# State-space coefficients made earlier, around the last heads of the recurrence, and the first query product in the common form

## The reference, cut to what matters

```python
# first layer: the modulated input times w_in, whose first columns are the queries
widths = (A_WIDTH, A_KV_WIDTH, A_KV_WIDTH, A_WIDTH, B_WIDTH, B_WIDTH, B_WIDTH, B_WIDTH)
q, k, v, g_a, xb, b_g, c_g, g_b = split_cols(modulate(x, shift, scale) @ w_in, widths)
# second layer: the recurrence's readout, head by head, then the output product
on = o * lax.rsqrt(jnp.mean(o * o, axis=-1, keepdims=True) + RMS_EPS) * g_norm
return (on.transpose(0, 2, 1, 3).reshape(B, L, H * dv) * jax.nn.silu(g)) @ w_out
# third layer: coefficients of the state-space mixer, from parameters alone
A = lax.complex(a_re, a_im)
dt = jnp.exp(log_dt)[:, None]
a_bar = jnp.exp(A * dt)
b_bar = ((a_bar - 1.0) / A)[..., None] * lax.complex(b_re, b_im)
bu = jnp.einsum('gpc,bsgc->bsgp', b_bar, u)
```

## Time and profile before

| | |
|---|---|
| median of 3 runs | 2365.18 us (2356.86 to 2365.84) |
| the profiled execution | 2361.89 us |
| its span, first to last instruction | 2360.1 us |
| mean granted TensorE clock | 0.974 |
| PE busy | 2196.2 us (93%) |
| DVE / ACT / POOL busy | 1076.5 / 668.6 / 801.4 us |

### The profile page before, as it was taken

How to read it: one execution, slowest core, us unless ns; L and a number is a source line. 1 busy time by engine, 2 the same in 40 slices (tenths; PEclk the granted TensorE clock), 3 DMA queues, 4 the chain that set the end, 5 groups by cost and what they waited for, 6 DMA issues and landing times. The chain is left out here.

```text
span 2360.1 us, 28075 instructions
## 1 busy us (share of the span) xinstructions
PE 2196.2 (93%) x11735; PEld 1766.8 (75%) x11735; DVE 1076.5 (46%) x1653; ACT 668.6 (28%) x1031; POOL 801.4 (34%) x382
## 2 busy tenths in 40 slices
PE   5999898989999999998978899999998999999997
PEld 3887777866676868886845678888887578888886
DVE  2114664653666565667896543111126664111114
ACT  3223223324545454642102432000013443010101
POOL 1422013401323322335400015544544255554453
PEclk7999999999999999998999999999999999999999
DMA  9332114422111111113111112323222222232322
GB/s 305 74 108 72 55 54 113 121 90 89 36 37 36 36 36 36 37 54 99 41 36 54 54 54 80 99 90 107 90 89 90 90 88 73 89 107 90 98 90 81
DMA packets 174797, 187.47 MB, mean 79 GB/s; under 512 B 25600, under 2 KB 153936, under 8 KB 174544
## 3 DMA queue, kind: packets, MB, share of 16 engines
q1 hardware_dynamic: 164720, 175.42, 23.8%
q10 hardware_dynamic: 9376, 8.16, 1.3%
q0 software_dynamic: 576, 2.10, 0.2%
HBM read 183.56 MB, written 2.10 MB: 79 GB/s over the span
## 5 line engine op out<-in xcount | busy, mean ns | idle before, releaser
L3022 POOL TENSOR_TENSOR weights_lo<-weights_raw,weights_hi 128x2048 fp32r<-128x2048 f32 (+1 forms) x102 | 462.5, 4534 | 851.1 <-ACT weights_hi L1443 654.9
L700 PE MATMUL ring<-input_hi,weights_hi 128*128 128x512 f32 x784 | 305.6, 390 | 3.3 <-POOL weights_lo L3022 3.0
L701 PE MATMUL ring<-input_lo,weights_hi 128*128 128x512 f32 x784 | 305.3, 389 | 0.0
L702 PE MATMUL ring<-input_hi,weights_lo 128*128 128x512 f32 x784 | 305.3, 389 | 0.0
L2864 DVE CAST weights_hi<-weights_raw 128x2048 fp32r<-128x2048 f32 (+1 forms) x72 | 87.7, 1218 | 366.1 <-PE ring L702 173.9
L3010 POOL TENSOR_TENSOR h_w<-h_p 128x512 f32<-128x512 f32 x56 | 72.6, 1297 | 413.9 <-PE ring L1031 307.8
L1004 PE MATMUL obank<-acts,weights_raw 128*128 128x512 f32 x384 | 176.6, 614 | 0.8 <-issue 0.8
L700 PEld LDWEIGHTS ring<-input_hi,weights_hi 128*128 128x128 f32 x784 | 147.2, 188 | 35.0 <-issue 4.6
L702 PEld LDWEIGHTS ring<-input_hi,weights_lo 128*128 128x128 f32 x784 | 147.2, 188 | 30.6
L701 PEld LDWEIGHTS ring<-input_lo,weights_hi 128*128 128x128 f32 x784 | 147.2, 188 | 30.2
L1013 PE MATMUL obank<-weights_raw,acts 128*128 128x256 f32 x640 | 143.2, 381 | 0.0
(11 more groups left out here) (474 smaller groups left out, 4409.8 us busy)
## 6 DMA issues: line engine op xcount, KB each, us to landing
weights_raw<-in_w_ada SPq DMA_DIRECT2D x24, 1024.0 KB, 5.3
weights_raw<-in_ffn_w_gate SPq DMA_DIRECT2D x22, 1024.0 KB, 5.2
weights_raw<-in_ffn_w_up SPq DMA_DIRECT2D x22, 1024.0 KB, 5.1
weights_raw<-in_w_in_c SPq DMA_DIRECT2D x20, 1024.0 KB, 5.2
weights_raw<-in_ffn_w_down SPq DMA_DIRECT2D x16, 1024.0 KB, 5.0
weights_raw<-in_w_in_ab SPq DMA_DIRECT2D x9, 1024.0 KB, 7.1
weights_raw<-in_ev_w_in SPq DMA_DIRECT2D x8, 1024.0 KB, 5.4
weights_raw<-in_od_w_in SPq DMA_DIRECT2D x8, 1024.0 KB, 5.6
```

Of the source, the lines that this page charges most:

```text
L700: pe.matmul(o, hi[:, k, ms], xh[:, k, t0:t0 + n], start=k == 0, stop=False)
L701: pe.matmul(o, hi[:, k, ms], xl[:, k, t0:t0 + n], start=False, stop=False)
L702: last = pe.matmul(o, lo[:, k, ms], xh[:, k, t0:t0 + n], start=False, stop=k == KD - 1)
L3022: pool.tensor_tensor(W_LO[slot][:, 0:kt, :], WR[:, slot, 0:kt, :], w_hi[:, 0:kt, :], ALU.subtract).then_inc(sem("w_lo"), 1)
```

## The change

It does two separate things. The first undoes the product of its own for `q0`: `q0` and `q1` both go through `split_f`, which waits for hi and lo weights first and then does the three matmuls k by k, each k of the first column tile behind its `h_lo`.

The second reorders DVE, ACT and POOL at the end of the recurrence. `s5_angles` loses its first part, which becomes `s5_columns`. The pieces of the diff are, in order: PE's list, ACT's list (between the root and `hi_upto("y11.0")` stand, as before, four loads of B and C and two of norm rows, which ACT issues), DVE's list, and POOL's.

```diff
-            hi, lo = split_chunk("q0", head_columns(0, 0), wait_lo=False)
...
-            split_f("q1", head_columns(0, 1), "a", True, H_HI, H_LO)
+            for c in range(2):
+                split_f(f"q{c}", head_columns(0, c),
+                        "a", True, H_HI, H_LO, "a", None if c else sem("h_lo"))
...
             heads_hi(0)
+            act.wait_ge(*read_of("s5rows"))
+            act.activation(pr(2), pr(2), ACT.Exp).then_inc(sem("s5_dt"), 1)
             heads_hi(1)
             heads_hi(2)
             hi_upto("y10.1")
+            act.wait_ge(sem("s5_ang"), 1)
+            act.activation(pr(5), pr(3), ACT.Exp)
+            act.activation(pr(2), pr(3), ACT.Exp, scale=float(CH))
+            act.activation(pr(6), pr(6), ACT.Sin)
+            act.activation(pr(7), pr(7), ACT.Sin).then_inc(sem("s5_sc"), 1)
             root(range(3, 4), 2)
...
+            hi_upto("y11.0")
             heads_hi(3)
-            pr = lambda k: SPR[:, k, :]
-            act.wait_ge(*read_of("s5rows"))
-            act.activation(pr(2), pr(2), ACT.Exp).then_inc(sem("s5_dt"), 1)
-            hi_upto("y11.0")
-            act.wait_ge(sem("s5_ang"), 1)
...
             hi_upto("y11.1")
...
                     heads_lo(1)
                     heads_lo(2)
-            inside(HEADS // HH - 1)
-            normed_heads(3)
-            heads_lo(3)
+            s5_angles()
+            inside(HEADS // HH - 1)
+            normed_heads(3)
+            s5_weights()
+            heads_lo(3)
+            s5_columns()
+            s5_inputs()
...
             tile_norms(y1_norm, 1, C_DIAG, HT, V_NPRE)
-            s5_weights()
-            s5_inputs()
...
+                lo_upto("y11.0")
+                s5_powers()
                 lo_upto("y11.1")
-                s5_powers()
                 s5_tables()
```

More of the change, by code:

```diff
@@ L587, in gemm_f, with split_chunk @@
                 used_with_unit()
-            def split_chunk(name, pieces, kt=KD, by="a", wait_lo=True):
+            def split_chunk(name, pieces, kt=KD, by="a"):
                 chunk(pieces, kt)
@@ L601, in split_chunk @@
                 pe.wait_ge(hi_done, len(hi_list))
-                if not wait_lo:
-                    return w_hi, w_lo
                 by_v = sum(x in split_no for x in LO_BY_V)
@@ L1776, in _ @@
             act.wait_ge(*fill_of(f"oi{LAST}"))
+            pr = lambda k: SPR[:, k, :]
             hi_upto("y10.0")
@@ L2510, in s5_angles, with s5_columns @@
             def s5_angles():
+                dve.wait_ge(sem("s5_dt"), 1)
+                mul(pr(3), pr(0), pr(2))
+                mul(pr(4), pr(1), pr(2))
+                sine_args(pr(4), pr(6), pr(7), pr(8), "s5_ang")
+                dve.wait_ge(sem("s5_ang"), 1)
+            def s5_columns():
                 dve.wait_ge(sem("s5_c_in"), 32)
@@ L2517, in s5_angles @@
                 ins.then_inc(sem("s5_cexp"), 1)
[L2518 to L2522, removed]
             def s5_weights():
```

## The result

The changed kernel takes 2371.19 us (median, 2367.03 to 2375.86), the kernel before in the same comparison 2364.52 us (2356.86 to 2365.84). The ratio is 1.0035 with a 95% interval from 1.0021 to 1.0049: about 8 us slower (5 to 12); the two medians alone differ by 6.7. The profiled execution took 2370.28 us, its span is 2368.5 us, against 2361.89 and 2360.1 before.

What follows compares the result with a forecast made beforehand. PE, busy 93% of the span, was taken as the bound, so only its waits could move the end. The terms 2.6 + 6.0 + 1.7 - 1.5 = +8.8 us, from 2365.2, gave 2374.0 us, range 2362 to 2381.

Steps and rivals of the forecast that it cites:

- Part 1: First query product: `q1` starts later, first column tile going k by k behind `h_lo`; +1.6 to +3.9 us, taken as +2.6.
- The clock cost that I added: First query product: second column tile may start at low clock, up to 1.7 us, plus 0.6 for the last three matmuls.
- Part 2: Output product, third tile: PE waits for L2389, delayed by angle operations that POOL stops; +6.0 us, bounds +1.4 and +6.0.
- the row that I had taken for the case: DVE's operation at 1078.81 in the earlier trace, taken as the same code beside the same POOL instruction: 4.57 us for 0.18.
- The clock behind it: Output product, behind the stall: PE's matmuls run at a low clock; +1.7 us, bounds 0 and 3.3.
- Rival C: Low clock lasts two stretches behind the output product's stall, and `q0`'s second column tile starts low; +11.7 us, chance 0.17.
- The rest of part 2: Last heads, joins, lo part of `y11.1`: reordered work hidden by PE's shift; cost 0, at worst +1 us at joins.
- 2.3 us to spare: POOL's lo part of `y11.1`, behind the powers, done at 1100.2; PE needs it at 1102.5, so cost 0.
- at worst 1 us: Second half's first joins: `s5_columns` and `s5_inputs` standing ahead of them cost 0, at worst +1 us.
- 3.7 us of cover: Last heads, without the stall: normed at about 1069.5, ahead of PE's turn at 1073.16, so 3.7 us of cover.
- Part 3: Behind the norm: PE's 1.53 us wait for DVE's powers vanishes; -1.5 us.
- Rivals A and B: Output product's third tile: A, small stall, +2.5 us, chance 0.18; B, no ring wait, faster, -1.4 us, chance 0.10.

Runs made afterwards that it cites:

- q_alone: Kernel before with only the first query product changed (both chunks through `split_f`); 2367.4 us, ratio to before 1.0003.
- pool_away: Changed kernel with ACT's hi part of `y10.1` behind the wait for the sine arguments, so POOL's lo part comes later; 2368.67 us, ratio to before 1.0010.
- reader_first: Changed kernel with DVE's `inside(3)`, the reader of `oo3`, ahead of `s5_angles`; ratio to before 1.0013.
- coef_alone: Changed kernel with the old `q0` product, so only the coefficients are moved; 2371.18 us, ratio to before 1.0023.
- pool_order: Changed kernel with POOL's old order: lo part of `y11.1`, then powers, then tables; ratio to before 1.0021.
- final: Changed kernel with old `q0`, `inside(3)` ahead of `s5_angles`, ACT's root and last heads earlier, readout directly behind DVE's powers; 2356.97 us, ratio to before 0.9970.
- final_old: `final` with POOL's old order (both lo parts, then powers, then tables); 2356.35 us, ratio to before 0.9964.
- mended: Changed kernel with the edits of `reader_first` and `pool_order` and the old `q0`; 2364.34 us, ratio to before 1.0009.
- readout_early: `mended` with `s5_readout` moved from behind the first scan step to directly behind DVE's `s5_powers`; 2355.06 us, ratio to before 0.9958.

## Why the prediction came out, point by point

The forecast was +8.8 us, 2374.0; measured were 2371.19 us and +8 (5 to 12) by the ratio. The stall, its place and what ends it came as forecast, and they are most of the loss. That the sum came so close is partly luck: the stages give some 4 us more than forecast, of which 3.6 I had not seen, and the two profiles differ by as much the other way where no code changed (below).

*Part 1, forecast +2.6.* `q1` starts 2.47 us later in after, 2.86 in `q_alone`. But 1.06 us of the first is POOL's later start, and 1.4 of the second (50.92 for 49.56), so the form costs 1.4 to 1.5 us, just under the lower end of 1.6. The clock cost that I added did not come. PE was at the low level at the first pieces (0.50 from 56 to 61), where it waited for POOL anyway, and at 1.00 from 62 on. In whole times the form's cost is unsettled.

*Part 2, forecast +6.0.* The wait is 6.16 us, at the third tile, ended by L2367, and a small operation is stopped for 4.38 us. `pool_away` and `reader_first` show that it takes both POOL's lo part and the order. Three small operations got ahead of POOL where I had two, and the fourth was stopped. It has one tile as its input and a constant; the one in the earlier trace rows had two tiles. So the row that I had taken for the case was another operation of the chain, and that one with a single tile is stopped as well is more than the earlier trace rows showed. The rule of the Trainium skill, SBUF — State Buffer, "SBUF: two separate sides" (an exclusive lock kept for the whole instruction), agrees with all of these rows if the one-input operation ran in a two-port mode, which no row here shows by itself: 4.38 us with POOL busy, 0.17 without.

*The clock behind it, forecast +1.7.* A is 8.72 us longer, 6.16 of it the new wait; what is left is 2.6 us, with the low level from 1063.68 to 1068.54. In `coef_alone`, with a wait of 5.72 us, it is 1.7. Rival C's mechanism (more than one stretch of 1.7 us) was half there; the bound of 3.3 held.

*The rest of part 2, forecast 0.* This failed at one place. I asked of POOL's powers only whether the lo part behind them would be late, and not what the tables behind *them* would stand beside: stage F, +3.6 us, back to +0.3 in `pool_order`. Everything else that I called hidden was hidden, but only under the stall. Without it the powers cost 6.7 us at `y11.1` (E of `final`), where I had 2.3 us to spare with a shift of 7.7. The columns and inputs ahead of the joins, for which I had at worst 1 us, cost 5.1 (D of `final_old`). And the last heads came late. There I had 3.7 us of cover, and had not counted that ACT's loads could keep it for 8.7 us (1067.71 to 1076.44) where before they took some 5.

*Part 3, forecast -1.5.* G is 1.7 us shorter in every kernel with the early coefficients, and then always 30.90. Against `q_alone`'s profile, where PE waits 2.75 us for the powers and the turns behind run at a low clock, G and H would be 4.6 us shorter. The earlier trace rows was one draw of a wait that varies (1.53 and 2.75 us in two traces of this order).

*A sign that was badly chosen.* I had written that a PE wait ended by `heads_lo(3)` would prove me wrong. After has one, 2.59 us, ended by L2402. But the kernel before has it too, 2.52 us, and it costs nothing new; the sign should have been a longer one, as the 6.93 us of `reader_first`.

*The sum again.* Term by term from the stages: 2.5 at `q1` (1.1 of it POOL's start) + 8.7 + 3.6 - 1.7 = +13.1 us; the spans differ by 8.4, the ratio says 8.3. Between them lie 4.5 us in stretches whose code is the same (`q1` to `y10` is 3.0 us shorter in after, the part behind H 1.5), which scatter by as much between any two profiles. So +8.3 is what the whole costs, and how much of the 13.1 beyond the stall is in it can't be said. That the tile norms' 3.6 us reach the end, for one, is read from the stages alone. Rivals A and B are out by the 6.16 us wait.

## What to carry to other kernels

Work moved into an engine's idle time must be laid beside the neighbours of all that is queued behind it, on every engine; here the largest cost that the forecast had missed, 3.6 us, came from POOL's tables, which no one had moved by themselves and which came to stand beside other DVE work. A stall hides later waits: mend it, and look again at each engine there, as ACT's queue (5.2 us) and POOL's powers (6.7 us) each gave a part of it back. A move that only empties an engine pays once later work is put into the hole. Here that took 15.4 us away behind it, 6 net of the 9.4 that it cost in front (by the stages; the medians of `mended` and `readout_early` differ by 9.3), and the emptying alone took 1.7.

## What the runs showed of the hardware

- A DVE operation of 128x16 with one tile as its input is stopped for the rest of a POOL operation as one with two: 4.38 us for 0.17. So are one of 128x1024 with the same tile twice (4.71 for 1.23) and the `c_diag` operations of 128x128 (0.98 on the mean for 0.29). Not stopped was the reader of `oo3`, with PSUM and one tile as inputs: before, it began 0.5 us inside POOL's operation and took its 1.23 us. Nor was BATCH_NORM_STATS2, with 0.69 us inside a POOL operation of 1.59.
- POOL's side stretches too: its 128x512 operations took up to 2.02 us beside the norms, 1.04 beside DVE operations that read PSUM and one tile, so two queues of such operations cost each other more than the one that is looked at shows.
- A load's issue on ACT can hold its queue for long: `s_cr<-in_s_c_im` took 1.69 us in before, 1.58 in after and 3.95 in `reader_first`, where it went out at another moment. The cause is open.
